# Making the negated weight copy on GpSimd instead of ScalarE

## The reference

```
h = RMSNorm(x);  p = h @ w_in            # 8 column groups of 1024: GLU a, GLU b, q, k, v, gate_conv, gate_attn
conv branch: GLU -> depthwise conv (31 taps) -> LayerNorm over channels -> SiLU -> @ w_pw2
attention:   stick-breaking, 16 heads of 64, causal, cumulative sums of log-sigmoids
x += (sigmoid(g_conv) * conv + sigmoid(g_attn) * attn) @ w_out
x += relu(RMSNorm(x) @ w_up)^2 @ w_down ;  final RMSNorm
```

## Time and profile before

| | |
|---|---|
| median of 3 runs | 1036.28 us (1036.01 to 1037.5) |
| profiled execution: its own time, its span | 1039.08 us, 1037.4 us |
| mean granted TensorE clock | 0.982 |
| TensorE matmul busy | 985.5 us, 95% |
| ScalarE busy | 608.0 us, 59% |
| VectorE busy | 499.2 us, 48% |
| GpSimd busy | 151.8 us, 15% |
| adding transfers w_lo<-w_raw | 136 of 512 KB, median 5.6 us from issue to landing |

### The profile page before, as it was taken

How to read it: one execution, slowest core, us unless ns; L and a number is a source line. 1 busy time by engine, 2 the same in 40 slices (tenths; PEclk the granted TensorE clock), 3 DMA queues, 4 the chain that set the end, 5 groups by cost and what they waited for, 6 DMA issues and landing times.

```text
span 1037.4 us, 20071 instructions
## 1 busy us (share of the span) xinstructions
PE 985.5 (95%) x7697; PEld 957.3 (92%) x7697; DVE 499.2 (48%) x841; ACT 608.0 (59%) x898; POOL 151.8 (15%) x308
## 2 busy tenths in 40 slices
PE   7899999999999999997989999999999999999995
PEld 6798989999898989897889999999999999999995
DVE  3548687877878787878452333222111122221122
ACT  5567776868777777776493455455433345463253
POOL 3211110111101111113011111111211111121110
PEclk8899999999999999999998999999999999999998
DMA  7665556464656556545747677878898858889543
GB/s 189 141 159 116 143 115 145 116 152 109 155 121 144 132 113 143 111 113 133 174 95 167 162 163 161 180 163 184 198 207 170 172 124 179 177 181 222 136 100 106
DMA packets 177330, 154.87 MB, mean 149 GB/s; under 512 B 5872, under 2 KB 158720, under 8 KB 177293
## 3 DMA queue, kind: packets, MB, share of 16 engines
q0 software_dynamic: 19584, 71.31, 38.3%
q1 hardware_dynamic: 147261, 78.21, 26.5%
q10 hardware_dynamic: 10448, 4.84, 1.7%
HBM read 75.97 MB, written 7.06 MB: 80 GB/s over the span
## 4 chain that ended last, share of the span: by engine, by line
issue 55%; PE 32%; DMA 4%; ACT 3%; POOL 2%; DVE 2%; SPq 1%; POOLq 0%; ACTq 0%; DVEq 0%
PE dense L432 32%; DMA w_raw<-in_w_in_dram 2%; DMA w_lo<-w_raw 2%; POOL tick L406 1%; ACT w_hi L738 1%; ACT w_lo L739 1%; POOL w_lo L407 0%; DVE sum_sq L1247 0%; ACT n L939 0%; ACT s_hi L941 0%; POOL r_lo L413 0%; DVE n L1080 0%; SPq L291 0%; PE z L697 0%; DVE s_lo L1254 0%
## 5 line engine op out<-in xcount | busy, mean ns | idle before, releaser
L432 PE MATMUL dense<-r_hi,w_hi 128*128 128x272 f32 (+1 forms) x1280 | 271.7, 294 | 14.5 <-DMA w_lo<-w_raw 7.3
L432 PE MATMUL dense<-r_hi,w_lo 128*128 128x272 f32 (+1 forms) x1280 | 267.8, 291 | 0.0
L432 PE MATMUL dense<-r_lo,w_hi 128*128 128x272 f32 (+1 forms) x1280 | 267.4, 290 | 0.0
L432 PEld LDWEIGHTS dense<-r_hi,w_hi 128*128 128x128 f32 x1280 | 202.9, 190 | 16.4 <-DVE kT L1185 8.0
L738 ACT ACTIVATE w_hi<-w_raw 128x1024 fp32r<-128x1024 f32 x136 | 142.9, 1051 | 103.9 <-PE dense L432 75.6
L432 PEld LDWEIGHTS dense<-r_hi,w_lo 128*128 128x128 f32 x1280 | 203.7, 190 | 0.0
L432 PEld LDWEIGHTS dense<-r_lo,w_hi 128*128 128x128 f32 x1280 | 202.9, 190 | 0.0
L1099 DVE SCALAR_TENSOR_TENSOR acc<-conv_in,cw_cur,acc 128x574 f32<-128x574 f32 x232 | 175.0, 812 | 0.4
L406 POOL TENSOR_TENSOR tick<-ones 128x1 f32<-128x1 f32 x136 | 32.4, 238 | 848.7 <-ACT w_lo L739 848.7
L739 ACT ACTIVATE w_lo<-w_raw 128x1024 fp32r<-128x1024 f32 x136 | 141.8, 1043 | 0.0
L432 PE MATMUL dense<-s_hi,w_hi 128*128 128x272 f32 x640 | 134.0, 291 | 6.4 <-DMA w_lo<-w_raw 5.2
(11 more groups left out here) (250 smaller groups left out, 1281.7 us busy)
## 6 DMA issues: line engine op xcount, KB each, us to landing
w_lo<-w_raw POOLq DMA_DIRECT2D x136, 512.0 KB, 5.6
w_raw<-in_w_in_dram SPq DMA_DIRECT2D x56, 512.0 KB, 5.2
w_raw<-in_w_up_dram SPq DMA_DIRECT2D x32, 512.0 KB, 4.5
w_raw<-in_w_down_dram SPq DMA_DIRECT2D x32, 512.0 KB, 6.3
w_raw<-in_w_pw_dram SPq DMA_DIRECT2D x8, 512.0 KB, 5.7
w_raw<-in_w_out_dram SPq DMA_DIRECT2D x8, 512.0 KB, 3.5
out_dram<-v_tok ACTq DMA_DIRECT2D x8, 256.0 KB, 5.3
out_dram<-k_tok ACTq DMA_DIRECT2D x8, 256.0 KB, 4.3
```

The costliest lines, as they stand in the source:

```text
L432: mm = nc.tensor.matmul(dense[:, slot, h, 0:half], w[:, wslot, k, :], m[:, k, c0 + h * half:c0 + (h + 1) * half], start=(k == 0 and n == 0 ...
```

## The change

The rounded copy alone raises `hi_done`. GpSimd makes w_lo as -1 times w_hi (the rounded tile, where ScalarE negated the raw one), waits for its own result, runs a second one-element addition and then issues the adding transfer.

```
-                nc.scalar.activation(w_hi[:, s], w_raw[:, s], ACT.Copy)
-                nc.scalar.activation(w_lo[:, s], w_raw[:, s], ACT.Copy, scale=-1.0).then_inc(hi_done, 1)
+                nc.scalar.activation(w_hi[:, s], w_raw[:, s], ACT.Copy).then_inc(hi_done, 1)
...
             def low(u, s):
                 pool.wait_ge(hi_done, u + 1)
                 pool.wait_ge(ticked, u + 1)
+                pool.wait_ge(ticked2, u + 1)
 
                 pool.tensor_tensor(tick[:], ones[:, 0:1], ones[:, 0:1], ALU.add).then_inc(ticked, 1)
+                pool.tensor_scalar(w_lo[:, s], w_hi[:, s].bitcast(F32), -1.0, None, ALU.mult).then_inc(negated, 1)
+                pool.wait_ge(negated, u + 1)
+
+                pool.tensor_tensor(tick2[:], ones[:, 0:1], ones[:, 0:1], ALU.add).then_inc(ticked2, 1)
                 pool.dma_start(w_lo[:, s].bitcast(F32), w_raw[:, s], accum_op=ALU.add).then_inc(lo_done[s], 16)
...
+        tick2 = sb("tick2", [P, 1])
+            pool.memset(tick2[:], 0.0).then_inc(ticked2, 1)
```

More of the change, by code:

```diff
@@ L245, in build @@
         zeroed, ticked = sem("zeroed"), sem("ticked")
+        negated, ticked2 = sem("negated"), sem("ticked2")
         POOL_LOWS = (3, 6)
```

## The result

The changed kernel is slower: 1057.12 us median (1056.17 to 1060.44, 4 runs) against 1036.89 (1036.01 to 1039.72, 4 runs) for the kernel before beside it. The ratio is 1.0196, 95% interval 1.0166 to 1.0226. The forecast of 1036.5 and its range of 1030 to 1048 are both missed. The profiled span is 1055.5 us, against 1037.4.

The account below looks back on a forecast made before the run. TensorE was taken as the bound, so only its waits (w_lo's adding transfer, q_low, kT) could move the time. The terms +1.0 - 1.4 + 1.3 - 1.5 + 0.8 summed to +0.2 us: 1036.5 us, range 1030 to 1048.

Parts of the forecast that it names:

- D: Duration of GpSimd's multiply over 128x1024, taken as 1.06 us, between 1.0 and 2.3.
- start: TensorE's second unit, waiting for w_lo of tile 1: transfer issued at 24.6 for 23.62, +1.0 us (+0.3 to +1.7).
- loop: Projection loop, 7 turns: q_low 0.95 us earlier, but the multiply holds the taps before kT; -0.2 each, -1.4 us.
- end of loop: Tile 51's 5.3 us wait: tick still behind the taps, then multiply and second tick; +1.3 us.
- LayerNorm, SiLU: Stretch where ScalarE's queue leads to TensorE: four copies leave, part lost to the multiply; -1.5 us.
- merge to the end: Merge to down projection: transfers 0.32 us later against median slack 1.6, showing only at late landings; +0.8 us.
- Path of one tile: From w_hi's start to the adding transfer's start: 1.47 + D = 2.53 us, for 2.21 before.
- rival three: In the loop the taps win the port: -5 us, 1031.5; chance 0.25 together with rival two.
- rival two: Tile 51's 5.3 us stall goes, as tick and multiply slip in: 1029 us; chance 0.25 together with rival three.
- Rival one: Long multiply, everywhere: D of 1.7 gives +11 us, 1047; D of 2.3 gives 1060; chance 0.37 with smaller forms.

Follow-up runs that it names:

- e_copy: Changed kernel with GpSimd copying w_hi into w_lo instead of multiplying by -1, negation left out: 1037.68 us, ratio 1.0004 to the kernel before.
- E_post: Kernel before, with GpSimd negating only the tiles from 51 on, as in the changed kernel: 1050.31 us, ratio 1.0142.
- e_direct: Changed kernel with one two-input GpSimd subtract forming w_lo, without multiply, second add and adding transfer: 1073.20 us, ratio 1.0338 to the kernel before.
- e_forms: Changed kernel with another GpSimd form per ring buffer (multiply, multiply in two pieces, copy, two-input subtract): 1047.9 us beside 1036.02 for the kernel before, one run.
- e_mix: Kernel before, but from tile 51 on one two-input GpSimd subtract forms w_lo, without adding transfer: 1023.19 us, ratio 0.9874.

## Why the prediction was wrong

**The step that failed is the first: D, "one GpSimd multiply", 1.06 us.** It is 2.77. Both bounds were taken from rows of other forms: the masks below, the two-input subtract above, as if two inputs must cost more than one. They don't here (1.92 against 2.77). My own reservation, "the mask rows being a different operation", was the case, and the upper end was no bound. With an instruction of D = 1.03 and everything else of the change kept (e_copy), the median is 0.6 us above the kernel before (interval -1.5 to +2.3) for +0.2 forecast. So the value of D is what missed. That the total comes out for its D is in part luck: by the table below, single terms were off by up to 3.5 us, in both directions.

The Trainium skill ("GPSIMD Engine Reference", section 3.1) gives 1.03 cycles an element for bodies of at most two operations: by estimate 0.9 us for 1024. The copy (1.03 us) agrees; the tensor-scalar form, 2.5 ns or by that page's clock three cycles a column, doesn't.

The terms, with what they measured in the changed kernel, and in e_copy, where D was as forecast (shift of TensorE's units against before, us):

| term | forecast | changed | e_copy |
|---|---|---|---|
| start | +1.0 | +6.2 | +1.7 |
| loop | -1.4 | +1.2 | -0.4 |
| end of loop | +1.3 | +0.9 | +0.2 |
| LayerNorm, SiLU | -1.5 | -1.3 | -3.1 |
| merge to the end | +0.8 | +11.4 | +4.3 |

E_copy's column is one execution of 1041.6 us, near the slowest of its ten (1034.86 to 1041.72, median 1037.68), against one of 1039.08 of the kernel before. It adds to +2.7, where the medians differ by 0.6, so a term of it is known to some 2 us at best. (E_post, whose start has the code of the kernel before, ended its start 2.1 us earlier than the kernel before did.)

**Path of one tile.** 1.47 + D: with D = 1.03 it gives 2.50, measured 2.50 in e_copy; with 2.77 it gives 4.24, measured 4.28. Right but for D.

**Start.** Two multiplies and two transfers follow each other on GpSimd, and ticks between them took 0.43 and 0.75 us for 0.19 beside the normalising: the second transfer started at 26.77 for 23.62, and landed 4.2 us later. TensorE's stall of 5.6 us on it then left a granted clock of 0.50 from 29.9 to 36.7, with 3.1 us of busy time in it, by estimate 1.6 us lost; the kernel before has none there, and I had priced none.

**Loop.** The waits came out as forecast: q_low 0.4 and kT 1.35 a turn, a tap stretched to 1.5. The multiply began 0.16 us before the first tap, so rival three (the taps win the port) fell. That the port is held for D - 0.13 was wrong: it is about 0.9 of the 2.77. This spared the loop: by my rule, breaking even at D = 1.28, it would have lost 7 x 1.5 = 10 us; it gained 2 in seven turns and lost 3 to the clock in two, which I had not priced. By the Trainium skill ("SBUF — State Buffer", "Who interferes with whom") two-input operations of VectorE conflict through the shared read interface with a GpSimd instruction that reads, while the lock for a whole instruction is told of VectorE's 2-port modes, which copies and tensor-scalar operations can enter. I had quoted the latter for all. The traces of the changed kernel agree with keeping the two apart: two first taps in the tensor-scalar form took 1.77 us at 298.91 against 0.95 in e_direct, held to the multiply's end, while the two-input operation before them was let go. But it isn't the whole: in e_forms one such tap ran its normal 0.52 us although it started 0.98 us into a 768-column multiply, and the next, 0.4 us later, was held to the end. No run says what decides it.

**End of the loop.** The tick was starved behind the taps as forecast, and the multiply went directly behind them:

```profile
488.37 5.31 POOL L410 TENSOR_TENSOR tick<-ones 128x1 f32<-128x1 f32 x1 [13.47 <-ACT w_hi L746]
493.66 2.76 POOL L411 TENSOR_SCALAR w_lo<-w_hi 128x1024 fp32r<-128x1024 f32 x1
496.51 0.19 POOL L414 TENSOR_TENSOR tick<-ones 128x1 f32<-128x1 f32 x1
496.64 0.89 POOL L415 DMA_DIRECT2D w_lo<-w_raw  x1
```

The stall grew from 5.3 to 7.3 us; rival two (it goes) fell. After it the unit ran shorter by 1.1, so the net was +0.9.

**LayerNorm and SiLU.** SiLU started at 527.60 for 523.17, 3.8 earlier against tile 51, where 2.3 was forecast; the longer path took 2.5 back at the transfer of 541, whose wait rose from 3.2 to 5.8.

**Merge to the end.** The term that paid: a path longer by 2.1 us against a median slack of 1.6. In the changed kernel TensorE waits there 10 times, 7.6 us, for 4 times and 3.0 before. One wait of 1.79 us, which ended at 605.8, was followed by 3.4 us at a granted clock of 0.50, so 1.7 us lost. That makes 6.3 of the 11.4. The rest is read from the units' times and not explained: the units with a wait are longer by some 0.3 us each beyond it, and some 2 us are spread over the others. In e_copy's execution this term was 4.3 and not 0.8: one wait grew from 1.8 to 2.7 us, and the unit behind it ran 1.5 longer at a clock of 0.50; I had priced no clock behind such waits.

**Rival one** had the mechanism and the direction, with 0.37. Its 1060 for D = 2.3 comes near 1057 by luck: D was longer still, and by its rule the loop would have lost 7 us at D = 2.3, where +1.2 was measured, all of it the lower clock.

## What to carry to other kernels

Price an operation of GpSimd by its form of instruction, from a row of that form; where no row has it, a row of another form bounds nothing, and the chance of a long one belongs in the forecast. An operation moved in front of a transfer costs whatever of its length the slack behind the landing doesn't cover (here 2.1 us of longer path against a median slack of 1.6); moved into the transfer's place, it can pay (e_mix). And ask of a GpSimd operation not only how long it is but how long it reads through the shared port: here two inputs held VectorE to the end. A longer stall can bring a stretch of lower clock with it, which belongs in its price (e_direct).

## What the runs showed of the hardware

- GpSimd, fp32 to fp32r, 128x1024, undisturbed: copy 1.03 us, two-input subtract or multiply 1.92 (from two different tiles 2.4), tensor-scalar 2.77 with a multiply, an add or a maximum. The tensor-scalar form took 2.5 ns a column and 0.2 us fixed (256 columns 0.85 us, 512 1.50, 768 2.12).
- A tensor-scalar operation of GpSimd held VectorE's two-input ones about 0.9 us of its 2.77, and so did a copy of 1.03. VectorE's tensor-scalar taps that started 1.4 to 1.7 us into it were held to its end, one that started 0.98 us into a 768-column piece was not held. A two-input operation of GpSimd of 2.4 us held VectorE's two-input ones for all of its length.
- A one-element operation of GpSimd waited 5.3 us behind back-to-back taps of VectorE in the changed kernel and 6.1 in e_mix; in both it ended with the last tap.
- TensorE's granted clock was 0.50 for 3.4 us behind two of seven stalls of 1.35 us and behind one of 1.79 (changed kernel), and for 6.8 us behind all seven of 4.8 (e_direct).
